# Seven block products instead of eight in the down units of both FFNs' first two parts

## What is computed

```
mod = (silu(c) @ w_ada + b_ada)          # nine vectors of 1024: shift, scale, gate of three blocks
x = x + 1/2 * gate1 * swiglu1(rmsnorm(x, g1) * (1 + scale1) + shift1)
x = x + gate_m * W_out(concat[conv_module, pool_mixer](W_in(mod(rmsnorm(x)))))
x = x + 1/2 * gate2 * swiglu2(rmsnorm(x, g2) * (1 + scale2) + shift2)
swiglu(x) = (silu(x @ w_gate) * (x @ w_up)) @ w_down
y = rmsnorm(x)
```

## Time and profile before

| | |
|---|---|
| median of 3 runs | 1045.11 us |
| the three runs | 1044.5, 1045.11, 1052.98 us |
| profiled execution, its own time | 1045.47 us |
| span of the profile | 1043.7 us |
| PE busy in the span | 98% |
| DVE, ACT, POOL busy | 57%, 43%, 47% |
| mean granted clock of TensorE | 0.981 |

### The profile page before, as it was taken

The page is one execution under the profiler, slowest core; times in us unless marked ns, Lnnn a source line. Parts: engine busy times, 40 slices in busy tenths (PEclk is TensorE's granted clock), DMA queues, the critical chain, the costliest instruction groups (busy, mean ns, idle before and its releaser), DMA issues.

```text
span 1043.7 us, 19650 instructions
## 1 busy us (share of the span) xinstructions
PE 1018.8 (98%) x7784; PEld 978.5 (94%) x7784; DVE 593.3 (57%) x1082; ACT 447.9 (43%) x733; POOL 485.6 (47%) x329
## 2 busy tenths in 40 slices
PE   8899999999999999999999999999999999999996
PEld 7699999999999999989976898999999999999996
DVE  4686423565424664659988436866235663356463
ACT  5565421355312553373343435555224553235432
POOL 2245442456433555546772033455535555445651
PEclk8999999999999999999999998999999999999997
DMA  8642465132361232443253322132322232213222
GB/s 338 223 182 93 151 242 202 50 113 82 129 235 41 97 107 96 145 178 146 82 132 149 157 81 82 50 113 85 118 82 81 85 119 101 102 44 120 87 76 91
DMA packets 21685, 127.46 MB, mean 122 GB/s; under 512 B 4192, under 2 KB 5344, under 8 KB 7008
## 3 DMA queue, kind: packets, MB, share of 16 engines
q1 hardware_dynamic: 15456, 96.06, 25.8%
q10 hardware_dynamic: 6144, 30.19, 7.9%
HBM read 123.06 MB, written 3.19 MB: 121 GB/s over the span
## 4 chain that ended last, share of the span: by engine, by line
PE 90%; issue 2%; DMA 2%; DVE 2%; ACT 2%; POOL 1%; SPq 0%; ACTq 0%; POOLq 0%; DVEq 0%
PE tile_a L463 21%; PE tile_b L463 20%; PE tile_b L517 15%; PE tile_a L517 15%; PE ada_ps L517 12%; DMA ada_raw<-w_ada 2%; PE ada_ps L435 2%; PE tile_a L706 2%; PE ada_ps L649 0%; PE stat_ps L575 0%; POOL w_lo L1670 0%; DVE sq L1285 0%; ACT x_hi L913 0%; PE stat_ps L720 0%; PE tile_a L708 0%
## 5 line engine op out<-in xcount | busy, mean ns | idle before, releaser
L1706 POOL TENSOR_TENSOR w_lo<-w_raw,w_hi 128x512 fp32r<-128x512 f32 x120 | 156.9, 1308 | 219.8 <-ACT w_hi L824 218.2
L1670 POOL TENSOR_TENSOR w_lo<-w_raw,w_hi 128x2048 fp32r<-128x2048 f32 x28 | 128.8, 4600 | 183.8 <-ACT w_hi L797 183.8
L1706 POOL TENSOR_TENSOR w_lo<-s_raw,w_hi 128x512 fp32r<-128x512 f32 x80 | 103.2, 1312 | 24.4 <-ACT w_hi L824 24.4
L824 ACT ACTIVATE w_hi<-w_raw 128x512 fp32r<-128x512 f32 x120 | 75.8, 632 | 69.8 <-PE tile_b L463 18.6
L797 ACT ACTIVATE w_hi<-w_raw 128x2048 fp32r<-128x2048 f32 x31 | 59.2, 1910 | 84.5 <-PE tile_b L463 82.4
L824 ACT ACTIVATE w_hi<-stat_ps 128x512 fp32r<-128x512 f32 x80 | 47.5, 596 | 81.5 <-DVE s_raw L1370 77.9
L463 PE MATMUL tile_a<-h_hi,w_hi 128*128 128x288 f32 x352 | 75.5, 296 | 0.0
L463 PE MATMUL tile_b<-h_hi,w_hi 128*128 128x288 f32 x352 | 75.0, 295 | 0.0
L463 PE MATMUL tile_a<-h_hi,w_lo 128*128 128x288 f32 x352 | 74.9, 294 | 0.0
L463 PE MATMUL tile_b<-h_lo,w_hi 128*128 128x288 f32 x352 | 74.9, 294 | 0.0
L463 PE MATMUL tile_b<-h_hi,w_lo 128*128 128x288 f32 x352 | 74.9, 294 | 0.0
(11 more groups left out here) (218 smaller groups left out, 2576.6 us busy)
## 6 DMA issues: line engine op xcount, KB each, us to landing
w_raw<-w_units SPq DMA_DIRECT2D x78, 1024.0 KB, 4.9
ada_raw<-w_ada ACTq DMA_DIRECT2D x28, 1024.0 KB, 6.9
ada_raw<-w_ada SPq DMA_DIRECT2D x8, 1024.0 KB, 6.7
x<-x_in SPq DMA_DIRECT2D x4, 576.0 KB, 5.9
y_out<-x SPq DMA_DIRECT2D x8, 288.0 KB, 2.4
conv_s<-conv_state SPq DMA_DIRECT2D x1, 480.0 KB, 5.8
conv_s_out<-conv_s ACTq DMA_DIRECT2D x1, 480.0 KB, 4.5
wp_raw<-w_pool SPq DMA_DIRECT2D x1, 256.0 KB, 7.1
```

Of the source, the lines that this page charges most:

```text
L824: nc.scalar.activation(slot(w_hi, i), source, ACT.Copy).then_inc(ready, 1)
L1670: nc.gpsimd.tensor_tensor(w_lo[:, side, :], w_raw[:, side, :], w_hi[:, side, :].bitcast(F32), ALU.subtract).then_inc(w_lo_ready, 1)
L1706: return nc.gpsimd.tensor_tensor(slot(w_lo, i), raw, slot(w_hi, i).bitcast(F32), ALU.subtract)
```

## The change

1. The four down units behind parts 0 and 1 of each FFN, sixteen units in all, become fast units. Part 2 (six tiles) keeps plain ones.
2. The hidden tiles of those parts are kept in seven slots of 288 tokens for each pair of tiles: four quarters and T1 to T4. For each pair DVE makes four sums of 288 columns (each from one operand in PSUM and one in SBUF, which is `kept` or an earlier sum), ACT rounds them and POOL splits them. T1 needs only the pair's even tile.
3. A down unit's results are added into x straight from PSUM: C11 by three DVE operations, C12 and C21 together by four, and C22 by one on ACT and two on POOL.
4. The products run in the order A11, S1, S2, A12, S3, S4, A22 (S2 and S1 are exchanged), block by block with the three passes inside; DVE's `low_s1` and `low_s2` and ACT's roundings follow that order, and `copy_a21` waits for both of DVE's lows.
5. Modulation blocks have no buffer of their own: they stand in free slots of `h_hi` and `h_lo`. Block 2 moves to FFN1's second unit: two quarters ahead of it, one between its tiles and one behind. Blocks 3 and 4 move to the plain down units of FFN1's last part, two quarters between the two tiles of each unit, through two slots. Of block 5 one quarter stands ahead of the norm's column sums and one behind them (with the transposes of block 4), and two between the chunks of the mixer's first unit.

The core of the diff, shortened (`fast_unit` and `ffn` are PE's, `window_sums` and `sum_t` DVE's, `residual_c22` POOL's, called ahead of the S4 low of the following unit):

```diff
 def fast_units():
-            out += range(u + (PLAIN_UPS if part == 0 else 0), u + n)
+            for i in range(PLAIN_UPS if part == 0 else 0, n + (DOWNS if part < FAST_PARTS else 0)):
+                out[u + i] = (f, part, i if i < n else i - n, i >= n)
...
+            def ada_slot(a):
+                if a < ADA_LATE:
+                    t = ada_lo[:, a % ADA_SLOTS]
+                elif a < ADA_MIX:
+                    t = (ada_hi, ada_lo)[a % 2][:, KH - 1]
+                else:
+                    t = ada_lo[:, 1 + a % ADA_SLOTS]
+                return t.rearrange("p (j n) -> p j n", j=2)
...
             def fast_unit(u, after_a12=None):
                 pe.wait_ge(s_lo_pool, 4 * o + 1)
+                bank_a_free(u)
+                product(u, P_A11, bank_a(u), True, (h_lo_ready, hidden - 1) if opens_down else None)
...
+                product(u, P_S1, bank_e(u), True, (ht_lo_ready, pairs - 3) if opens_down else None)
...
+                product(u, P_S2, bank_b(u), True, (ht_lo_ready, pairs - 2) if opens_down else None)
                 pe.wait_ge(s_lo_pool, 4 * o + 2)
                 pe.wait_ge(p1_copied, o + 1)
+                product(u, P_A12, bank_a(u), False, (h_lo_ready, hidden) if opens_down else None)
...
                 pe.wait_ge(u2_ready, o + 1)
+                product(u, P_S3, bank_b(u), False, (ht_lo_ready, pairs - 1) if opens_down else None)
...
+            def window_sums(u):
+                f, part, i, down = UNIT_KIND[u]
+                following = u + 1 if u + 1 in FAST else None
+                opens, opens_down = u in FIRST_FAST, down and i == 0
+                hide = not opens and not is_down(u - 1)
+                if opens:
+                    plain_hidden(u - 1, 1)
+                else:
+                    add_c21_c12(u - 1)
+                if following and not opens_down:
+                    sum_s1(following)
+                if hide:
+                    hidden(u - 1)
+                elif not opens:
+                    residual_pair(u - 1)
+                if opens_down:
+                    hidden_t2(u - 1)
+                    add_p15(u)
+                    hidden_sums(u - 1, 3)
+                    hidden_low(u - 1)
+                    sum_s1(following)
+                if following:
+                    sum_s3(following)
...
+                if not opens_down:
+                    add_p15(u)
+                add_u2(u)
...
+                if following:
+                    sum_s2(following)
+                    sum_s4(following)
+                add_c22(u)
...
+                if following:
+                    low_s1(following)
+                if down:
+                    residual_c11(u)
+                if following:
+                    low_s2(following)
...
+            def sum_t(pair, n, a, b):
+                if pair:
+                    dve.wait_ge(ht_lo_ready, 4 * (pair - 1) + n)
+                nc.vector.tensor_tensor(t1_raw[:, n - 1, :], a, b, ALU.subtract).then_inc(ht_sum, 1)
...
+            def residual_c22(u):
+                pool.wait_ge(c22_scaled, d + 1)
+                nc.gpsimd.tensor_tensor(kept_tail, tail, rows, ALU.mult).then_inc(c22_step, 1)
+                pool.wait_ge(c22_step, d + 1)
+                nc.gpsimd.tensor_tensor(xm, xm, kept, ALU.add).then_inc(c22_added, 1)
...
             def ffn(f, norm):            
+                    ada_products(2, 0, 2)
+                    unit(up + 1, lambda: ada_products(2, 2, 3))
+                    ada_products(2, 3)
...
+                down_unit(down, n, before + n, lambda: ada_products(3, 0, 2))
+                down_unit(down + 1, n, before + n, lambda: ada_products(3, 2, 4))
+                ada_turn(3)
+                down_unit(down + 2, n, before + n, lambda: ada_products(4, 0, 2))
+                down_unit(down + 3, n, before + n, lambda: ada_products(4, 2, 4))
```

More of the change, by code:

```diff
@@ new lines, in ffn @@
+                up, down = FFNS[f][0][2], FFNS[f][-1][3]
+                load_table(ACT.Silu)
+                plain_gate(up)
+                hi_t(f, 1, X_T1, t1_raw)
+                copy_a21(up + 2)
+                plain_round(up, 0)
+                hi_t(f, 2, X_T2, t2_raw)
+                hi_a11(up + 2)
+                hi_a12(up + 2)
+                hi_s1(up + 2)
+                hi_s2(up + 2)
+                plain_gate(up + 1)
+                hi_t(f, 3, X_T3, t3_raw)
+                hi_s3(up + 2)
@@ L1006, in squares @@
+                copy_a21(up + 3)
+                hi_s4(up + 2)
+                for u in fast_of(f):
+                    if f == 0 and u == FFNS[f][-1][2] + 1:
+                        ada_load(ADA_LATE)
+                        ada_load(ADA_LATE + 1)
+                    window(u, down)
+                gate_c12(down - 1)
+                round_hidden(down - 1)
+                split_hi(down + 1)
+                squares(norm_after, down)
             def squares(n, first_unit):
@@ L1451, in down_and_squares @@
                     add_square(n, 2 * i + 1)
-            def window_sums(u, i, n, before, ends, late):
-                following = u + 1 if i + 1 < n else None
-                if ends == "fast":
+                    if n == 1 and i == 1:
+                        mod_evacuate(3)
+            def window_sums(u):
+                f, part, i, down = UNIT_KIND[u]
+                following = u + 1 if u + 1 in FAST else None
+                opens, opens_down = u in FIRST_FAST, down and i == 0
+                hide = not opens and not is_down(u - 1)
+                if opens:
+                    plain_hidden(u - 1, 1)
+                else:
@@ L1464, in window_sums @@
                 if following:
                     sum_s3(following)
-                if ends == "fast":
-                    hidden_low(u - 1, i - 1, before)
+                if opens:
+                    dve.wait_ge(h_hi_ready, hidden_before(u))
+                    sum_t2(pair_of(u) - 1, tile_b[:, 1, 0:HALF])
+                    sum_t3_t4_hidden(pair_of(u) - 1, tile_b[:, 0, 0:HALF], tile_b[:, 1, 0:HALF], full[:, 0, HALF:])
+                elif hide and not opens_down and has_sums(u - 1):
+                    hidden_sums(u - 1)
@@ new lines, in ffn @@
+                _, _, up, _, before = FFNS[f][0]
+                sum_t1_t2(f)
+                plain_hidden(up, 0)
+                second_half_low(up + 1)
+                low_t(f, 1, X_T1, t1_raw)
+                sum_s1(up + 2)
+                sum_s3(up + 2)
+                sum_s2(up + 2)
+                sum_s4(up + 2)
+                plain_low(0, before)
+                if f:
+                    mod_evacuate(8)
+                first_t1(up)
+                low_s1(up + 2)
+                low_t(f, 2, X_T2, t2_raw)
@@ L1541, in ffn @@
+                low_s2(up + 2)
+                sum_t3_t4(f)
+                low_t(f, 3, X_T3, t3_raw)
+                for u in fast_of(f):
+                    window_sums(u)
+                down = FFNS[f][-1][3]
+                add_c21_c12(down - 1)
+                hidden(down - 1)
+                hidden_low(down - 1)
+                dve.wait_ge(c22_added, DOWNS_OF_FFN * (f + 1))
+                down_and_squares(down, 2 * KD * f, gate, norm_after)
                 inverse(norm_after)
@@ L1547, in _ @@
             ffn(0, GATE[0], 1)
+            mod_evacuate(4)
             apply_norm(1)
```

642 lines of the change are left out of this document (369 added, 273 removed).

## The result

The changed kernel took 1036.79 us in the median (1034.16 to 1040.23), the kernel before beside it 1049.67 (1041.75 to 1055.94). The ratio is 0.9874, with a 95% interval of 0.9856 to 0.9892: 1.3% faster, by 12.9 us. That is 5.8 us above the 1031 that was forecast, and 0.8 outside the range. The profiled execution took 1038.07 us, with a span of 1036.3.

What follows compares the result with a forecast made beforehand. TensorE, busy 98% of the span, was taken as the bound. From the profiled 1045.5 us, -25.3 + 3.1 - 1.5 - 0.2 + 0.3 - 0.7 + 0.3 + 1.9 + 1.7 + 6.0 = -14.4 gave 1031, range 1017 to 1036.

Steps and rivals of the forecast that it cites:

- Products: Sixteen down units lose 12 matmuls each, 192 in all, on PE's path: -25.3 us.
- Does it fit in a window: New DVE, ACT and POOL work fits in the 11.2 us window; nothing booked for twelve of sixteen down windows.
- First down window: First down window of a part, four times: PE waits about 0.75 us for `add_u2` at S3, +3.1 in all.
- Block 2 at the start: FFN1's start: two moved quarters stand where PE waits 1.5 us for ACT's silu, -1.5.
- The wait of 0.4 for `full`: FFN2's first fast window: the lows ahead of this wait now come later, -0.2, bounds -0.4 and +1.
- The loads of blocks 3 and 4: FFN1's last part: pairs land about 9 us after last use, against 9.6 between uses; +0.3 booked.
- rival (d): Seven-product down windows: DVE becomes the bound, its small operations blocked by POOL lows; slower, 1060 at 13 us windows; chance 0.06.
- Rival (c): FFN1's last part and norm: three late pairs at 2 us and full 3.4 of clock; 1038, chance 0.12.
- Block 5 in the norm and the clock: Norm and mixer start: quarters moved (-0.7, +1.9), transposes (+0.3), one more half-clock stretch (+1.7): +3.2.
- The pace in FFN2: FFN2: a new wait ends the 0.1300 us matmul pace, 0.1333 from there for 1820 matmuls, +6.0.

Runs made afterwards that it cites:

- both edits that take the lateness away: Changed kernel with modulation loads issued ahead of the squares (ratio 0.9783), or with the 64-column add taking an operand from PSUM (ratio 0.9788), each alone.
- the early loads: Changed kernel with ACT issuing the modulation loads behind FFN1's last part ahead of the square, not behind it: 1027.56 us, ratio 0.9783.
- the five kernels without them: Changed kernel with `add_u2` ahead of the two long sums, alone (ratio 0.9839) or with other edits (0.974, 0.9723, 0.9758, 0.9733).

## Why the prediction was wrong, by its own steps

**Products, -25.3.** Right. 192 matmuls are gone, and up and down windows run on PE without a gap but for the 0.46 us at the first down window (the rows of 137 to 193 and 787 to 874 us). From the first fast window to the first of FFN1's last down units the changed kernel takes 314.7 us (68.6 to 383.2) against 339.6 (65.7 to 405.2): -24.9, of which 96 matmuls are 12.8 and the rest mostly the twelve quarters of blocks 2 to 4 that now stand ahead of that stretch or behind it.

**Does it fit in a window.** Right: the twelve down windows that follow another one have no wait. An up window holds 58.89 x 11.2/87 = 7.6 us of DVE, 6.8 of ACT and 7.8 of POOL; forecast were 7.5, 6.7 and 8.0. A POOL low of 288 columns took 0.85 us on average (64 on L1986), where 0.8 had been taken between bounds.

**First down window, +3.1.** The mechanism and the place were right: the wait is on `add_u2` at S3, four times. The order as forecast ended at 7.05 us behind the opening; it ended at 6.7. So the size was 1.9, not 3.1, and the edit that moves the sum removes it.

**Block 2 at the start, -1.5.** The wait of 1.5 us for silu is gone, as forecast. The size can't be read: the first fast window opens at 68.57 and 67.62 us in two profiles of the changed kernel (with 3.8 us of block 2 ahead of it), and at 65.67, 65.02 and 67.70 in three of the kernel before. The wait of 0.4 for `full` in FFN2's first fast window, booked at -0.2, is gone too.

**The loads of blocks 3 and 4, +0.3.** This is the step that failed. The text booked "up to 2 us until ACT has squared and issued", and then 9 us to landing against 9.6 between uses. In fact the square was held, and the load was issued 4.1 us behind the start of the quarter's use and 3.1 behind its end (388.97, 390.02, 393.08), and took 10.06 to PE's release. Late were the loads used at 400.42 (0.65), 403.19 (1.70), 426.57 (0.79), 428.93 (1.30) and, for block 5, for whose first load nothing had been booked, 436.77 (1.79): 6.2 us. With what hangs on it in the norm, 9 us; both edits that take the lateness away gain that.

The rows that say so were in hand. The earlier trace rows shows the add held for 2.83 us, and the earlier trace rows that a square waits for this add; the add ahead of that last square is a short one, but the square before it shows the whole delay in the kernel before:

```profile
439.84 2.97 DVE L1437 TENSOR_TENSOR x<-x,gated 128x64 f32<-128x64 f32 x1
...
442.84 0.69 ACT L891 ACTIVATE sq<-x 128x576 f32<-128x576 f32 x1 [3.29 <-DVE x L1437]
```

The hold was used for rival (d), on the sixteen seven-product windows, where the new operations are safe from it, and not for the last part's down units, in which it had always stood. Harmless there as long as nothing but a square hung behind it, it became costly when DMA issues were put behind that square. Rival (c), late loads of blocks 3 and 4 with more half clock, had the place right: 1038 was its time, 0.12 its chance, and the profiled execution took 1038.07. It was to decide from a landing of over 9 us, and the load of 393.08 took 10.06. But it had no reason for the lateness, and where it had three late pairs of 2 us, two pairs were late (4.4 us) and one load of block 5 (1.8): that the time agrees so closely is in part luck.

**Block 5 in the norm and the clock, +3.2.** From the column sums' start in the chain to the mixer's first matmul the kernel before took 7.63 us:

```profile
445.67 2.32 PE stat_ps L575 x20
```

and the changed one 10.89 (437.84 to 448.73), with PE's last wait at 3.4 us where 3.6 was forecast. From the end of FFN1's last block product to the mixer's second unit it is 24.22 us before (443.80 to 468.02) and 31.47 after (434.98 to 466.45): 7.25 more, of which 1.8 is the late load, so 5.4 against the 3.2 booked. With the early loads the same way takes 28.12 us (430.74 to 458.86), 3.9 more than before. So by these profiles 3.9 is this term's own size, with the new wait for the sigmoid in it (0.8 in that profile), and the other 1.5 hangs on the late loads. How much of the rest is clock and how much the quarters was not measured apart.

**The pace in FFN2, +6.0.** The number came out: from FFN2's first seven-product window to its last block product it is 357.3 us before (671.05 to 1028.35) and 352.5 after (669.25 to 1021.74), -4.8 where -12.5 + 6.0 + 1.5 = -5.0 was forecast. (The trace of the kernel before has some 2450 matmuls at 0.1300 and not 2334; that would make the term some 0.2 larger.) What was wrong was to take the pace for the kernel's own. In the later two profiles of the kernel before the same stretch takes 365.3 us, and in the second profile of the changed kernel 352.5 again: beside a profile at 0.1333 the change gains 12.8 us, which is the products' 96 x 0.1333. That is also why the first two profiled executions are only 7.4 us apart (1045.47 and 1038.07) and the medians 12.9: the forecast started from an execution below the median, and this term happened to make up for it. That a wait can end the pace of 0.1300, as the forecast had it, the second profile shows. Whether the change keeps it out stays open. Its new waits for `add_u2` are not what does: the five kernels without them don't show it either.

**The sum again.** Taken from the median of 1049.67 and without the pace, the forecast's sum is 1049.67 - 20.4 = 1029.3; with 5.9 more for the loads, 2.2 for the norm (1.5 of it by the loads) and 1.2 less for the first down windows it is 1036.2, and 1036.79 was measured. The corrections are read from single executions, so an agreement to 0.6 us is better than they can promise.

## What to carry to other kernels

A DMA issue is due at the time at which its engine reaches it: before loads are put behind an instruction of a compute engine, follow what this instruction waits for, and what that one is held by. A delay that the profile shows as harmless is harmless only for what hangs on it now; when work is moved behind it, it must be priced again. A pace seen in one profiled execution is a property of that execution until a second one shows it, and so is a base time that comes with it. And where the times of two kernels overlap, the length of a stage between two landmarks may still tell them apart: 2.2 and 2.8 us were read that way here.

## What the runs showed of the hardware

DVE's add of 128x64 with both inputs in SBUF took 3.59 us under a POOL operation on 128x2048, until that one ended, and 0.23 us with one input in PSUM. The hold is passed on to the next operation with two inputs in SBUF (2.29 us in place of 0.76).

TensorE showed two paces at full clock for the same alternation of weight loads and 288-column matmuls, 0.1300 and 0.1333 us, and went from one to the other at a wait of 0.4 to 0.7 us, in either direction; what selects it stays open. Of three profiles of the kernel before, one has the faster for 318 us, one for 9 us, and one not at all. Its times spread over 14.2 us beside the changed kernel (1041.75 to 1055.94), and eight of its 62 times in all comparisons lie under 1046; those of the changed kernel spread over 6.1, those of no variant over 6.2. That the pace causes this spread was not tested.

A 1 MB load of `ada_hi` landed in 4.9 us in the median with the early loads, which start 3.5 us ahead of the other queue's (390.00 and 393.52), and in 7.1 in the changed kernel, where both start together (392.69 and 392.74). That the distance between the starts is the cause wasn't tested by itself.
